# An RWKV scan in which VectorE adds the old state that identity products had loaded into PSUM

## The chip, the cores and the metric

The kernel runs on one core of a Trainium2 chip. The metric is the device time of one execution in microseconds (us), here the median of three runs. Five engines work beside each other, each in the order of its own program, and meet at semaphores: TensorE (PE in the profile; PEld is its loading of weights), VectorE (DVE), ScalarE (ACT), GpSimd (POOL) and SyncE (SP), which issues the transfers. [...]

## The reference

The program is one layer of a hybrid block: normalised and modulated tokens (256 context tokens, then 256 latent ones, width 2048) go through a projection, two token mixers (RWKV-7 and GLA), a gated merge, and a feed-forward part. The change is in the RWKV scan, 16 heads of 64 channels, once forward and once backward. Step by step it is

```python
def step(s, inp):
    sa = einsum('bhvk,bhk->bhv', s, kk_t)
    s = s * w_t - sa[..., None] * (kk_t * a_t) + v_t[..., None] * k_t
    return s, einsum('bhvk,bhk->bhv', s, r_t)        # the output, for latent tokens only
```

The latent scans start from the context scans' final states.

## The kernel before

The kernel is a row of blocks, each with a program for every engine, and a block starts when all engines are through with the one before. The scan is one block (`phase_rwkv_scan`); the mix and the feed-forward part follow in the next.

The scan works on chunks of 64 tokens, 8 for each direction: chunks 0 to 3 are context, 4 to 7 latent. A *half* is one chunk of one direction (`_f` forward, `_b` backward), all 16 heads; there are 16 halves, taken forward, backward, forward, and so on. A half of the context goes through these steps, a latent half through some more:

- `prepare` to `prepare3` (VectorE, with exponentials `es`, `e` from ScalarE): running sums of log decays (`b`) and the scaled operands `s12`, `q12`.
- `scores1`, `scores2`, `scores3`: products of them on TensorE (into `pb`, `pa`, `pb`; the third, wide one is for latent halves only, L1707), masked by VectorE into `first`, `t2` and `r12` (the page calls these `t_f`, `r_f`).
- `open`, four `stage`s and `close`: the inverse of a triangular matrix by doubling. In each, VectorE transposes (`turned`, L1457) and masks (`step`, L1459), ScalarE copies (`grown`), and TensorE multiplies (`grow`, L1737).
- `inverse`, `rhs`, `u`: TensorE forms the inverse, the right side (from the old state `S`) and their product u (L1780); ScalarE copies each (L1603 the right side, L1608 u).
- `from_state`, `output` (L1789, L1800, latent halves): the output in `pb`, copied into `b_y` by ScalarE or, in the last chunks, added to it by VectorE (L1516).
- `state`: the new state. Before the change, `u_step` first issues two products of the unit matrix with `S` (L1775) into the second half of each bank of `pa`; the state product (L1810) adds to them there; VectorE multiplies the whole by the decay over the chunk, `e_end` (L1507), and writes `S`.

The order of each engine is written out by hand. In `run_tensor`, `run_vector` and `run_scalar` a loop over n goes through the halves, and a line such as `latents("state", 2)` does that step for half n − 2 if it is a latent one (`context` and `every` likewise). So an engine works on two or three halves in turn, and a step waits for its semaphores with all that stands behind it on its engine. `ends` makes `e_end`; `forward` makes `e`.

Of the kernel before, what the change touches and what calls it, by code (L numbers as in the profile page):

```python
# [20 lines left out]
P = 128  # L21
# [5 lines left out]
C = 64  # L27
# [1207 lines left out]
def phase_rwkv_scan(nc, A, out, env, y_sum, yb, raw):  # L1235
# [3 lines left out]
    U8 = PAIRS  # L1239
# [3 lines left out]
    def sm(name, d):  # L1243

        if (name, d) not in names:
            names[name, d] = sem(f"s_{name}_{'fb'[d]}")
        return names[name, d]

    with ExitStack() as st:
# [126 lines left out]
        with nc.Block() as block:  # L1376
# [31 lines left out]
            def _(dve):  # L1408
# [108 lines left out]
                def run_vector(step):  # L1517
                    for n in range(-1, len(HALVES) + 3):
                        every, context, latents = calls(step, n)
                        latents("close", 3)  # L1520
                        context("stage", 2, 1)
                        latents("open", 2)
                        latents("prepare1", 1)
                        every("prepare2", 1)
                        context("stage", 2, 2)
                        latents("stage", 2, 1)
                        every("prepare", 0)
                        latents("stage", 2, 2)
                        latents("output", 3)
                        context("stage", 2, 3)  # L1530
                        latents("prepare3", 1)
                        latents("stage", 2, 3)
                        every("state", 3)
                        latents("scores1", 1)
                        context("stage", 2, 4)
                        context("scores1", 1)
                        latents("stage", 2, 4)
                        every("scores2", 1)
                        context("open", 1)
                        latents("scores3", 1)  # L1540
                        context("close", 2)
                        context("prepare1", 0)
# [4 lines left out]
            def _(act):  # L1547
# [61 lines left out]
                def run_scalar(step):  # L1609
                    for n in range(-1, len(HALVES) + 3):  # L1610
                        every, context, latents = calls(step, n)
                        every("u", 2)
                        context("stage", 1, 3)
                        context("prepare", -1)
                        latents("stage", 1, 2)
                        latents("output", 2)
                        context("stage", 1, 4)
                        latents("prepare", -1)
                        context("close", 1)
                        context("tokens", 0)  # L1620
                        latents("stage", 1, 3)
                        context("flips", 0)
                        context("forward", -1)
                        latents("stage", 1, 4)
                        latents("forward", -1)
                        context("ends", 0)
                        latents("close", 1)
                        latents("tokens", 0)
                        context("stage", 0, 1)
                        latents("flips", 0)  # L1630
                        every("halve", 1)
                        every("rhs", 1)
                        latents("ends", 0)
                        context("stage", 0, 2)
                        latents("stage", 0, 1)
# [14 lines left out]
            def _(pe):  # L1650
# [1359 lines left out]
```

## Time and profile before

| | |
|---|---|
| median of 3 runs | 2209.29 us (2205.83 to 2209.69) |
| profiled execution | 2204.9 us, span 2203.3 us |
| scan block | 966.6 to 1246.0 us of the span |
| context halves, about | 976.6 to 1096 us |
| latent halves, about | 1096 to 1231 us, then a tail |
| granted TensorE clock, mean | 0.966 |

The span is the profiled execution from its first to its last instruction. Times in the rows count from its start. A recorded group such as "MATMUL ... x32" is a run of products of one line: 16 products of 64 columns, which the trace shows as two each in this type.

### The profile page before, as it was taken

What the parts mean: (1) busy time and instruction counts of PE and PEld (TensorE: products, weight loads), DVE (VectorE), ACT (ScalarE), POOL (GpSimd) and SP (SyncE); (2) the same over time, 40 slices, a digit from 0 to 9 for tenths busy, and PEclk for the clock granted to TensorE, in tenths of its full rate; (3) what the DMA queues carried; (4) which work ended last, traced back from release to release, by engine and by line L of the source; (5) the groups of instructions that cost most, each with busy time, mean ns of one, the idle gap of its engine ahead of it and who ended that gap; (6) DMA issues with size and microseconds to landing.
All of it is one profiled execution on the core that took longest, in us unless ns stands there. A gap on an engine that the chain in (4) does not pass through costs nothing. (4 is left out here: it accounts for less than half of the span.)

```text
span 2203.3 us, 37509 instructions
## 1 busy us (share of the span) xinstructions
PE 2052.1 (93%) x16171; PEld 1691.6 (77%) x16171; DVE 1344.8 (61%) x1258; ACT 811.2 (37%) x890; POOL 277.2 (13%) x135
## 2 busy tenths in 40 slices
PE   7679999999899999977889899989999999999998
PEld 3258888888678886656778688878888888878886
DVE  3465666665627737768888677475656565654444
ACT  1232212123063125625555555343434334333333
POOL 0242213223113304411000020000000000000000
PEclk9689999999989999989999999999999999999999
DMA  9989888987173459997544477535555555555553
GB/s 333 348 285 328 306 323 283 328 309 229 40 221 95 108 145 267 311 244 177 104 89 85 58 230 299 193 105 191 190 190 190 190 187 187 179 206 195 191 191 115
DMA packets 406658, 454.09 MB, mean 206 GB/s; under 512 B 108062, under 2 KB 357262, under 8 KB 389246
## 3 DMA queue, kind: packets, MB, share of 16 engines
q1 hardware_dynamic: 398912, 441.04, 62.5%
q10 hardware_dynamic: 7614, 11.10, 1.4%
q8 instruction: 105, 1.72, 0.3%
q14 instruction: 27, 0.22, 0.0%
HBM read 413.89 MB, written 38.22 MB: 205 GB/s over the span
## 5 line engine op out<-in xcount | busy, mean ns | idle before, releaser
L215 DVE TENSOR_TENSOR f_w_lo<-t_w_raw,f_w_hi 128x2048 fp32r<-128x2048 f32 x132 | 302.3, 2290 | 307.0 <-ACT f_w_hi L209 307.0
L270 PE MATMUL pf<-h,f_w_hi 128*128 128x512 f32 x1320 | 463.9, 395 | 0.0
L209 ACT ACTIVATE f_w_hi<-t_w_raw 128x2048 fp32r<-128x2048 f32 x132 | 253.2, 1918 | 445.7 <-PE pf L270 283.6
L269 PE MATMUL pf<-h,f_w_lo 128*128 128x256 f32 x1320 | 367.4, 278 | 0.3 <-DVE h L2666 0.3
L270 PEld LDWEIGHTS pf<-h,f_w_hi 128*128 128x128 f32 x1320 | 247.6, 188 | 54.3
L269 PEld LDWEIGHTS pf<-h,f_w_lo 128*128 128x128 f32 x1320 | 248.3, 188 | 4.6 <-DVE h L2666 0.6
L209 ACT ACTIVATE p_w_hi<-h_w_raw 128x2048 fp32r<-128x2048 f32 (+1 forms) x52 | 96.4, 1901 | 338.8 <-DVE stage L726 252.1
L261 PE MATMUL p_in<-h,p_w_lo 128*128 128x512 f32 (+1 forms) x512 | 199.3, 389 | 0.0
L259 PE MATMUL p_in<-h,p_w_hi 128*128 128x512 f32 (+1 forms) x512 | 199.3, 389 | 0.0
L260 PE MATMUL p_in<-h,p_w_hi 128*128 128x512 f32 (+1 forms) x512 | 199.2, 389 | 0.0
L858 DVE SCALAR_TENSOR_TENSOR late_acc<-h_of_x,siluc,late_acc 128x2048 f32<-128x2048 f32 x60 | 161.9, 2698 | 38.5 <-DMA h_of_x<-in_ada_w 36.9
L2885 PE MATMUL d_out<-f_w_hi,hid 128*128 128x512 f32 x704 | 177.4, 392 | 2.9 <-DVE f_w_lo L215 2.9
L215 POOL TENSOR_TENSOR p_w_lo<-h_w_raw,p_w_hi 128x2048 fp32r<-128x2048 f32 (+1 forms) x26 | 123.5, 4753 | 312.5 <-ACT p_w_hi L209 312.5
L2885 PEld LDWEIGHTS d_out<-f_w_hi,hid 128*128 128x128 f32 x704 | 132.7, 189 | 31.2 <-DVE f_w_lo L215 3.6
L904 PE MATMUL po<-h_of_x,gate_w 128*128 128x256 f32 x576 | 133.1, 389 | 2.3 <-ACT g_vt L1995 0.9
L904 PEld LDWEIGHTS po<-h_of_x,gate_w 128*128 128x128 f32 x576 | 110.9, 196 | 19.6 <-issue 2.3
L260 PEld LDWEIGHTS p_in<-h,p_w_hi 128*128 128x128 f32 (+1 forms) x512 | 95.7, 187 | 20.6
L261 PEld LDWEIGHTS p_in<-h,p_w_lo 128*128 128x128 f32 (+1 forms) x512 | 95.7, 187 | 20.4
L259 PEld LDWEIGHTS p_in<-h,p_w_hi 128*128 128x128 f32 (+1 forms) x512 | 95.7, 187 | 20.3
L270 PE MATMUL p_in<-h,p_w_hi 128*128 128x512 f32 x300 | 106.3, 397 | 0.0
L215 DVE TENSOR_TENSOR m_w_lo<-t_w_raw,h 128x2048 fp32r<-128x2048 f32 x32 | 74.8, 2348 | 47.0 <-ACT h L209 47.0
L904 PE MATMUL r_pg<-h_of_x,gate_w 128*128 128x256 f32 x416 | 94.7, 384 | 7.1 <-DMA gate_w<-in_w_in 4.1
(408 smaller groups left out, 3332.1 us busy)
## 6 DMA issues: line engine op xcount, KB each, us to landing
h_of_x<-in_ada_w SPq DMA_DIRECT2D x64, 1024.0 KB, 5.0
h_w_raw<-in_w_in SPq DMA_DIRECT2D x51, 1024.0 KB, 7.2
t_w_raw<-in_ffn_w_gate SPq DMA_DIRECT2D x44, 1024.0 KB, 5.0
t_w_raw<-in_ffn_w_up SPq DMA_DIRECT2D x44, 1024.0 KB, 5.1
t_w_raw<-in_ffn_w_down SPq DMA_DIRECT2D x44, 1024.0 KB, 4.9
h_w_raw<-in_ada_w SPq DMA_DIRECT2D x32, 1024.0 KB, 8.8
gate_w<-in_w_in SPq DMA_DIRECT2D x32, 1024.0 KB, 5.8
t_w_raw<-in_w_out SPq DMA_DIRECT2D x16, 1024.0 KB, 6.3
```

The lines of the kernel that those rows point to most:

```text
L209: act.activation(self.hi[:, m % self.S, 0:w], self.raw[:, s, 0:w], ACT.Copy)\
L215: eng.tensor_tensor(self.lo[:, m % self.S, 0:w], self.raw[:, s, 0:w], b32(self.hi[:, m % self.S, 0:w]), ALU.subtract)\
L259: pe.matmul(o, wh, xh, start=first, stop=False)
L260: pe.matmul(o, wh, xl, start=False, stop=False)
L261: return pe.matmul(o, wl, xh, start=False, stop=last)
L269: pe.matmul(hi, wl, x[:, 0, k, :], start=False, stop=False)
L270: return pe.matmul(both, wh, x[:, :, k, :], start=False, stop=last)
L858: dve.scalar_tensor_tensor(out=acc, in0=self.raw[:, t % 2], scalar=scalar, in1=acc, op0=ALU.mult, op1=ALU.add).then_inc(self.used, 1)
L904: mm = pe.matmul(self.banks[t % nb][:, 0:SEQ], self.raw[:, slot, k * P:(k + 1) * P], self.hx[:, k, :], start=k == 0, stop=k == KT - 1)
L2885: return pe.matmul(pd[4 * b + c][:], hid[:, part, t, b * P:(b + 1) * P], v[:, t % 2, 512 * c:512 * c + 512], start=first, stop=stop)
```

## The change

Three things change. (1) `u_step` no longer issues the identity products; the state product starts its sums anew (`start=True`), and VectorE first adds the old state to it (`S` + `pa` into `S`, with a new semaphore `sadd`), waits for that, and then multiplies `S` by `e_end`. (2) `scores2`, which writes `pa`, waits for the addition and not for the multiplication. (3) The steps of the three compute engines are written in a new order. For most halves this gives the same order as before, since the loop's turn starts at another step (the numbers of halves back are shifted with it).

```diff
@@ state (VectorE) @@
                     dve.wait_ge(sm("st", d), c + 1)
+                    dve.tensor_tensor(by_parity(S[d][:]), by_parity(S[d][:]), narrow(pa[d], 1), ALU.add).then_inc(sm("sadd", d), 1)
+                    dve.wait_ge(sm("sadd", d), c + 1)
                     dve.wait_ge(sm("e_end", d), c + 1)
-                    dve.tensor_tensor(by_parity(S[d][:]), narrow(pa[d], 1), e_end[d][:].rearrange("p (u b) -> p b u", b=2)
-                                      .unsqueeze(3).broadcast_to([P, 2, U8 // 2, C]), ALU.mult).then_inc(sm("S", d), 1)
+                    dve.tensor_tensor(S[d][:], S[d][:], e_end[d][:].unsqueeze(2).broadcast_to([P, U8, C]), ALU.mult)\
+                       .then_inc(sm("S", d), 1)
@@ scores2 (TensorE) @@
-                        pe.wait_ge(sm("S", d), c)
+                        pe.wait_ge(sm("sadd", d), c)
@@ u_step (TensorE) @@
                     pe.wait_ge(sm("inverse", d), c + 1)
-                    goes_on = c != LAST
-                    if goes_on:
-                        for b in range(2):
-                            at = b * BANK + BANK // 2
-                            pe.matmul(pa[d][:, at:at + BANK // 2], eye[:],
-                                      S[d][:].rearrange("p (u b) c -> p b u c", b=2)[:, b], start=True, stop=False,
-                                      skip_group_check=True)
                     pe.wait_ge(sm("rhsc", d), c + 1)
...
-                        last = pe.matmul(by_token(pa[d], j, h), tok(xt[d], j, h), tok(rhs[d], j, h), start=not goes_on,
-                                         stop=True, skip_group_check=True)
+                        last = pe.matmul(by_token(pa[d], j, h), tok(xt[d], j, h), tok(rhs[d], j, h), start=True, stop=True)
@@ state (TensorE) @@
                         last = pe.matmul(by_feature(pa[d], j, h, 1), st12[d][:, 2 * j + h, :], uv[d][:, block_of(j, h), :],
-                                         start=False, stop=True, skip_group_check=True)
+                                         start=True, stop=True)
@@ run_tensor, two of its lines @@
-                        latents("grow", 1, 3)
-                        latents("scores2", 0)
...
+                        latents("scores2", -1)
...
+                        latents("grow", 0, 3)
@@ run_scalar, two of its lines @@
-                        latents("output", 2)
...
-                        latents("prepare", -1)
...
+                        every("prepare", -1)
...
+                        latents("output", 2)
```

On VectorE, in the context halves, the order stays but for the state. The piece is from a forward half: `pa` is the PSUM tile with the new state's product, `turned_b` and `step_b` belong to the next half, which is backward.

```order
 L1457 STREAM_TRANSPOSE turned_b<-pa 128x512
 L1459 TENSOR_TENSOR step_b<-turned_b,masks 128x512
-L1507 TENSOR_TENSOR S_f<-pa,e_end_f 128x2x4x64
+L1506 TENSOR_TENSOR S_f<-S_f,pa 128x2x4x64
+L1509 TENSOR_TENSOR S_f<-S_f,e_end_f 128x512
 L1457 STREAM_TRANSPOSE turned_b<-pb 128x512
 L1459 TENSOR_TENSOR step_b<-turned_b,masks 128x512
```

One instruction has become two, and the fourth transpose stands behind both.

On VectorE, in a latent half, before (`q_f` is the scaled operand of the half ahead, `first_f` its first selection):

```order
L1457 STREAM_TRANSPOSE turned_b<-pa 128x512
L1459 TENSOR_TENSOR step_b<-turned_b,masks 128x512
L1454 TENSOR_TENSOR q_f<-rc_f,e_f 128x8x64
L1507 TENSOR_TENSOR S_f<-pa,e_end_f 128x2x4x64
L1473 COPY_PREDICATED first_f<-masks,pb 128x512
L1457 STREAM_TRANSPOSE turned_b<-pb 128x512
```

and now:

```order
L1454 TENSOR_TENSOR q_f<-rc_f,e_f 128x8x64
L1457 STREAM_TRANSPOSE turned_b<-pa 128x512
L1459 TENSOR_TENSOR step_b<-turned_b,masks 128x512
L1506 TENSOR_TENSOR S_f<-S_f,pa 128x2x4x64
L1509 TENSOR_TENSOR S_f<-S_f,e_end_f 128x512
L1473 COPY_PREDICATED first_f<-masks,pb 128x512
```

The addition stands between the third mask and the first selection. (The scaling of `q_f` is in front of the transpose here, at the first latent half; in the later ones it was so before.)

On TensorE, from the right side of a latent half on, before (L1737 is the growth, L1689 the first scores, L1697 the second, L1707 the third):

```order
L1766 MATMUL pb<-S_b,q_b 64x64 x16
L1737 MATMUL pa<-first_f,step_f 64x64 x16
L1775 MATMUL pa<-S_b,ident 128x256 x2
L1780 MATMUL pa<-rhs_b,xt_b 64x64 x16
L1737 MATMUL pb<-grown_f,step_f 64x64 x16
L1810 MATMUL pa<-uv_b,st_b 64x64 x16
L1737 MATMUL pa<-grown_f,step_f 64x64 x16
L1689 MATMUL pb<-s_b,q_b 64x64 x16
L1737 MATMUL pb<-grown_f,step_f 64x64 x16
L1697 MATMUL pa<-q_b,s_b 64x64 x16
L1707 MATMUL pb<-q_b,s_b 128x64 x16
```

and now:

```order
L1772 MATMUL pb<-S_b,q_b 64x64 x16
L1743 MATMUL pa<-first_f,step_f 64x64 x16
L1779 MATMUL pa<-rhs_b,xt_b 64x64 x16
L1743 MATMUL pb<-grown_f,step_f 64x64 x16
L1808 MATMUL pa<-uv_b,st_b 64x64 x16
L1743 MATMUL pa<-grown_f,step_f 64x64 x16
L1695 MATMUL pb<-s_b,q_b 64x64 x16
L1703 MATMUL pa<-q_b,s_b 64x64 x16
L1743 MATMUL pb<-grown_f,step_f 64x64 x16
L1713 MATMUL pb<-q_b,s_b 128x64 x16
```

The identity products are gone, and the second scores have moved ahead of the third growth. In context halves TensorE's order loses the identity products and is otherwise the same. On ScalarE, `forward` stands earlier and `ends` later in context halves, and in latent halves `prepare` (the exponential `es`) has moved ahead of the second copy and the output's copy.

## Rows read from the trace of the kernel before

**Rows 1.** The page: the chain that ended last, share of the span by line.

```profile
PE pf L270 13%; PE d_out L2885 11%; PE pf L269 7%; PE o_out L2799 3%; PE m_up L270 1%; DMA t_w_raw<-in_w_gla_up 1%; PE pf L267 1%; PE m_up L269 1%; DVE m_w_lo L215 1%; PE pf L268 0%; ACT f_w_hi L209 0%; DVE f_w_lo L215 0%; PE o_turned L2839 0%; DMA t_w_raw<-in_ffn_w_gate 0%; ACT h L209 0%
```

**Rows 2.** Busy time by window: the whole scan, context stage, latent stage.

```profile
core 0: us, PE busy (x) PEld busy (x) DVE busy (x) ACT busy (x) POOL busy (x), PEclk, DMA share, GB/s
966.60:1246.00 279.40, 232.68 (x7160) 205.50 (x7160) 222.69 (x323) 141.19 (x246) 7.71 (x4) 0.95 0.51 107
976.60:1096.00 119.40, 92.97 (x2977) 80.29 (x2979) 99.05 (x138) 64.99 (x114) 6.72 (x2) 0.93 0.69 150
1096.00:1231.00 135.00, 120.85 (x3878) 109.22 (x3877) 111.88 (x159) 69.52 (x122) 0.00 (x0) 1.00 0.37 72
```

**Rows 3.** Timeline of one context half: start, duration, instructions, idle before and releaser.

```profile
start us, us, engine line op out<-in xcount [idle before <-releaser]
1046.05 0.71 DVE L1457 STREAM_TRANSPOSE turned_f<-pa 128x512 f32<-128x512 f32 x1
...
1047.76 0.60 ACT L1603 ACTIVATE rhs_b<-pb 128x512 f32<-128x512 f32 x1
...
1048.16 1.13 PE L1775 MATMUL pa<-S_b,ident 128*128 128x256 f32 x4
...
1049.22 1.09 PE L1780 MATMUL pa<-rhs_b,xt_b 64*64 64x64 f32 x30
1049.73 1.22 DVE L1431 TENSOR_TENSOR_SCAN b_f<-keep,ld_f 128x512 f32<-128x512 f32 x1
...
1050.42 1.21 ACT L1608 ACTIVATE uv_b<-pa 64x512 f32<-64x512 f32 x2 [0.70 <-PE pa L1780]
1050.99 0.72 DVE L1457 STREAM_TRANSPOSE turned_f<-pa 128x512 f32<-128x512 f32 x1
...
1051.77 1.15 PE L1810 MATMUL pa<-uv_b,st_b 128*64 128x64 f32 x32 [0.93 <-ACT uv_b L1608]
...
1052.98 0.69 DVE L1507 TENSOR_TENSOR S_b<-pa,e_end_b 128x512 f32<-128x512 f32 x1 [0.55 <-PE pa L1810]
...
1053.69 0.72 DVE L1457 STREAM_TRANSPOSE turned_f<-pb 128x512 f32<-128x512 f32 x1
...
1059.79 0.71 DVE L1457 STREAM_TRANSPOSE turned_b<-pa 128x512 f32<-128x512 f32 x1
```

**Rows 4.** Timeline of one latent half.

```profile
1192.79 0.69 DVE L1459 TENSOR_TENSOR step_b<-turned_b,masks 128x512 f32<-128x512 f32 x1
...
1193.79 0.27 PE L1737 MATMUL pb<-grown_b,step_b 64*64 64x64 f32 x2
...
1194.36 1.10 PE L1789 MATMUL pb<-q_f,S_f 64*64 64x64 f32 x32
...
1195.58 0.69 PE L1800 MATMUL pb<-r_f,uv_f 128*64 128x64 f32 x14
...
1196.85 0.74 PE L1800 MATMUL pb<-r_f,uv_f 128*64 128x64 f32 x18 [0.59 <-issue]
...
1197.63 0.69 DVE L1516 TENSOR_TENSOR b_y<-b_y,pb 128x512 f32<-128x512 f32 x1 [1.51 <-PE pb L1800]
...
1198.83 0.71 DVE L1457 STREAM_TRANSPOSE turned_b<-pa 128x512 f32<-128x512 f32 x1
...
1199.58 0.69 DVE L1459 TENSOR_TENSOR step_b<-turned_b,masks 128x512 f32<-128x512 f32 x1
1200.19 0.68 DVE L1507 TENSOR_TENSOR S_f<-pa,e_end_f 128x512 f32<-128x512 f32 x1
...
1200.79 0.73 DVE L1473 COPY_PREDICATED first_f<-masks,pb 128x512 f32<-128x512 uint32 x1
...
1201.58 2.00 PE L1707 MATMUL pb<-q_f,s_f 64*128 64x64 f32 x32
```

**Rows 5.** TensorE's waits, 976 to 1246: us in total, times, longest.

```profile
PE pb L1689 <- issue: 8.7, 5, 4.5
```

**Rows 6.** Busy time in one window, columns as in rows 2.

```profile
1024.00:1028.00 4.00, 3.55 (x80) 3.43 (x80) 2.74 (x4) 0.78 (x2) 2.23 (x1) 0.50 1.09 348
```

More of the change, by code:

```diff
@@ L1611, in run_scalar @@
                         every, context, latents = calls(step, n)
-                        every("u", 2)
+                        latents("rhs", 2)
+                        context("ends", 1)
+                        latents("stage", 1, 1)
+                        context("stage", 1, 2)
+                        context("u", 2)
                         context("stage", 1, 3)
-                        context("prepare", -1)
+                        latents("u", 2)
+                        every("prepare", -1)
+                        context("stage", 1, 4)
+                        context("forward", -1)
                         latents("stage", 1, 2)
                         latents("output", 2)
-                        context("stage", 1, 4)
-                        latents("prepare", -1)
+                        latents("stage", 1, 3)
+                        latents("ends", 0)
+                        latents("stage", 1, 4)
+                        latents("close", 1)
+                        latents("forward", -1)
                         context("close", 1)
+                        latents("tokens", 0)
+                        latents("flips", 0)
                         context("tokens", 0)
-                        latents("stage", 1, 3)
                         context("flips", 0)
[L1623 to L1628, printed above, removed]
                         context("stage", 0, 1)
-                        latents("flips", 0)
                         every("halve", 1)
[L1632 to L1635, printed above, removed]
+                        context("rhs", 1)
                 run_scalar(dict(prepare=prepare, forward=forward, ends=ends, output=output,
@@ L1815, in run_tensor @@
                         every, context, latents = calls(step, n)
-                        context("grow", 1, 2)
-                        latents("grow", 1, 1)
-                        latents("from_state", 2)
-                        latents("output", 2)
-                        context("state", 2)
-                        latents("grow", 1, 2)
-                        latents("state", 2)
-                        latents("scores1", 0)
-                        context("grow", 1, 3)
-                        context("scores1", 0)
-                        context("scores2", 0)
-                        latents("grow", 1, 3)
-                        latents("scores2", 0)
-                        latents("scores3", 0)
                         context("grow", 1, 4)
@@ L1837, in run_tensor @@
                         latents("flips", 0)
-                        every("inverse", 1)
-                        every("rhs", 1)
+                        context("inverse", 1)
+                        context("rhs", 1)
+                        latents("inverse", 1)
+                        latents("rhs", 1)
                         context("grow", 0, 1)
@@ L1842, in run_tensor @@
                         every("u", 1)
+                        latents("grow", 0, 1)
+                        latents("from_state", 1)
+                        context("grow", 0, 2)
+                        context("state", 1)
+                        latents("output", 1)
+                        latents("grow", 0, 2)
+                        latents("state", 1)
+                        latents("scores1", -1)
+                        context("grow", 0, 3)
+                        latents("scores2", -1)
+                        context("scores1", -1)
+                        latents("grow", 0, 3)
+                        context("scores2", -1)
+                        latents("scores3", -1)
                 run_tensor(dict(scores1=scores1, scores2=scores2, tokens=tokens, flips=flips, scores3=scores3,
```

27 lines of the change are left out of this document (15 added, 12 removed).

## Prediction

> **What bounds the kernel now.** I read the last chain first. Its largest pieces are products of the feed-forward part, and no line of the scan stands in it [rows 1]. That does not make the scan free: the phases are separate blocks, each waits for the one before it, and the chain reaches back only to the block behind the scan. Whatever the scan gives or takes goes on one to one. The scan is 279.4 us long, from 966.6 to 1246.0 (the bounds of its stages are those of [rows 2], with 10 us of start in front and 15 us of tail behind).
>
> Next the busy times by stage. In the context stage TensorE is busy for 92.97 of 119.40 us and VectorE for 99.05; in the latent stage TensorE for 120.85 of 135.00 and VectorE for 111.88 [rows 2]. Neither engine is full, so I need the order within a half (one chunk of one direction), and read the timeline of one half in each stage.
>
> In the context half, the reader should see that VectorE has one real pause, 0.55 us before it forms the state at 1052.98, and that from 1053.69 to 1059.79 it goes from one instruction to the next for 6.10 us without a listed wait. TensorE pauses 0.93 us for ScalarE's copy of u. The half takes 13.74 us, 1046.05 to 1059.79 [rows 3]. In the latent half TensorE runs nearly without a pause up to the output product; VectorE waits 1.51 us for that product. Then comes a tight stretch: third transpose 1198.83, its mask 1199.58, state 1200.19, first selection 1200.79, and TensorE's wide product at 1201.58, which needs that selection and on whose end VectorE's next masking waits [rows 4].
>
> **The change, part by part.** *The identity products go.* In both halves they hold TensorE for 1.06 us (1048.16 to 1049.22) before the u product; 14 of 16 halves have them, 14.8 us of TensorE in all. What is late next is the copy of the right side on ScalarE, which u needs. Context: it ends at 1047.76 + 0.60 = 1048.36, and with the 0.14 us that lies between ScalarE's end and TensorE's start elsewhere (1050.42 + 1.21 to 1051.77) u starts at 1048.50, 0.72 earlier, not 1.06 [rows 3]. In the latent half I take the same 0.7 us for u; there, as will be seen, it is not u that decides.
>
> *VectorE gets an addition in 14 halves.* Its form is not in the scan's state step before, but the same shape with one operand in PSUM is in the output sum at 1197.63, 0.69 us [rows 4]. What counts is start to start. Behind an instruction whose result is not needed at once the next starts 0.60 to 0.61 us later (1199.58 to 1200.19 to 1200.79); where the next needs the result it is 0.75 us (1198.83 to 1199.58) [rows 4]. The multiplication needs the sum, so the added price is 0.75 us of VectorE. The bounds are 0, if it lies in the 0.55 us pause and that pause was longer than it looks, and 0.75. I take 0.75, since an instruction of this kind has never cost less than 0.60 here. The multiplication now reads SBUF alone; the mask at 1199.58 does too and takes 0.69 us, the state from PSUM 0.68 [rows 4], so nothing changes.
>
> The Trainium skill (VectorE: DVE Perf Modes, "The DRAIN you can't avoid") says that a semaphore after each VectorE operation costs nothing over one after the last. These rows do not agree: 0.75 against 0.61 where the result is waited for. By the rule the addition would cost 0.61 and the sum below would be up to 1 us lower.
>
> *Context half, walked through.* u at 1048.50 ends at 1049.6; the copy of u starts when ScalarE is through with what stands before it, 1049.72 (1050.42 less the 0.70 of idle), and ends at 1050.93; the state product starts at 1051.07 and is 0.70 earlier. VectorE: second mask and scan stay, since they waited for TensorE's first growth, not for u. The third transpose moves from 1050.99 to 1050.95. Its mask starts at 1051.70, the addition at 1052.31 (the state product has ended at 1052.22), the multiplication at 1053.06, the fourth transpose at 1053.67. Before it was at 1053.69 [rows 3]. The 0.55 us pause has been turned into the addition, and what follows is VectorE's full 6.10 us. Gain: 0.02 to 0.04 us a half; over 7 halves 0.3 us. TensorE's saving has become waiting.
>
> *Latent half, walked through.* This half has a stop within TensorE's output product (0.59 us listed); without it the product, 1.15 us long where it runs through as the state product of the same shape does [rows 3], would have ended at 1196.73 and not at 1197.59, and the work behind it stood 0.86 us earlier: third transpose at 1197.97, wide product at 1200.72 [rows 4]. After the change the growth behind u, before at 1193.79, waits for VectorE's mask, which ends at 1193.48, so it starts at 1193.54, 0.25 earlier only; the product from the old state at 1194.11, output at 1195.33, third transpose 1197.72, all 0.25 gained. Then mask 1198.47, addition 1199.08, multiplication 1199.83, first selection 1200.44, which ends at 1201.17. The wide product starts at 1201.22 where it would have stood at 1200.72: 0.50 later, the addition's 0.75 less the 0.25. TensorE's new order adds no more: the second scores, now ahead of the third growth, wait for the addition's end (1199.77), start at 1199.8, growth at 1200.4, both done by 1201.1. But this uses up all the room there was. From the wide product on, VectorE's masking, transposes and scaling follow one another up to the next half, so 0.50 is the price of a half. The seven halves in which an addition meets latent scores make +3.5 us.
>
> *The other moves.* ScalarE has pauses of 0.7 us before the copy of u in the context half [rows 3]; moving the exponentials and the end decays fills such pauses. DMA triggers hang on the same steps as before. Where the stages meet, VectorE's scaling is placed ahead of a transpose, once; 1.2 us at most, in either direction. I count zero.
>
> **Sum.** −0.3 + 3.5 = +3.2 us. The profiled execution took 2204.9 us (span 2203.3 and 1.6 around it), so it would be 2208.1. The profiled one lies 4.4 us below the median 2209.29 of the runs shown; on the median the forecast is 2212.5. About 0.2%, or 4.4 us, is what a measurement of this kernel can tell from no change, so the likeliest outcome is the same or barely slower.
>
> **Rivals.** *A: TensorE sets the latent half and the addition hides (faster).* For it: 120.85 of 135 us busy [rows 2], and TensorE's stops within its own products, 8.7 us at the first scores alone, one of them 4.5 [rows 5]. The new wait for the addition comes right behind those scores, and a stop there would vanish in it. Against: the walk. Price: 7 × 1.06 = 7.4 us gained, 2201.9; with the other 4.2 us of those stops 2197.7.
>
> By the Trainium skill (Runtime: NRT & Kernel Launch, "Instruction fetch mechanics") fetching instructions is hidden behind their issue. Rows with a product broken off in its middle and no engine to wait for [rows 4, 5] do not fit that; by the rule the 4.2 us would not be there to gain.
>
> *B: VectorE sets every half (slower).* One mechanism: ScalarE's copy of u does not come the 0.7 us earlier, so the 0.55 us pause before the state stays and the addition is put behind it. Price 14 × 0.75 = 10.5 us, 2219.8. It decides as soon as the state product in the context half starts no earlier than before. For it: VectorE is the fuller engine of the context stage. Against: the copy had been waiting 0.70 us for TensorE.
>
> *C: TensorE's clock falls more often (slower).* In 1024 to 1028 the granted clock was 0.50, that is 1.2 GHz, and 80 products took 3.55 us, behind 4.5 us without products [rows 5, 6]. With identity products gone, TensorE idles more in the context stage. At 2.4 GHz the same work takes half of 3.55 us, so such a stretch costs 1.8 us; two falls of two such stretches each make 7.1 us, 2216.4, and three 2219.9. Against: pauses of 0.5 us in the regular halves did not bring it.
>
> **Chances.** The forecast 0.43 (its own range 2208 to 2216), A 0.24, B 0.16, C 0.12, stops moved to other places by the shorter program 0.05, either way. Faster by over 0.2%: A and half the last, 0.26. Slower: B, C, and the upper edge of the forecast, 0.36. The same: 0.38. Range 2201 (most of A) to 2221 (B).
>
> **What would show it.** Step by step, in the profile after: the addition about 0.69 us and 0.75 us ahead of the multiplication; context halves of 13.7 us with no pause before the state; TensorE pausing 0.5 us before the second growth in them; in latent halves the wide product 3.5 us behind the third transpose (2.75 before) and TensorE waiting for the addition before the second scores. A pause before the addition would speak for B, latent halves a microsecond shorter for A, more stretches at 0.50 for C. The forecast is wrong if the scan is more than 5 us off 282.6 us.

## The result, and the profile after

The changed kernel took 2216.57 us (median of 8 runs, 2210.53 to 2225.08), the kernel before 2209.32 on the same chip: ratio 1.0037, 95% interval 1.0022 to 1.0052. It is slower by 7 us; the forecast was 2212.5, inside a range of 2201 to 2221. The time lies in the range, but 0.6 us above the 2208 to 2216 that the forecast itself was given: the range reached so far up for the sake of the rivals. The profiled execution took 2214.55 us (span 2212.8), 9.6 us more than that of before. Of this some 2.4 us is the choice of executions, since that of before was quicker than all eight that were timed, 4.4 us below their median, and this one is 2.0 below its own. The scan grew from 279.4 to 289.7 us, so it explains all of it, and it lies 7.1 us off the 282.6 that the sum gave: by the prediction's own bound of 5 us the sum was wrong in this execution.

The same stages as in [rows 2], shifted with the scan's start and end:

```profile
core 0: us, PE busy (x) PEld busy (x) DVE busy (x) ACT busy (x) POOL busy (x), PEclk, DMA share, GB/s
965.30:1255.00 289.70, 225.28 (x7104) 201.07 (x7105) 235.38 (x337) 142.01 (x247) 7.71 (x4) 0.94 0.50 103
975.30:1097.20 121.90, 86.56 (x2921) 75.10 (x2921) 106.81 (x144) 64.92 (x114) 6.72 (x2) 0.93 0.67 147
1097.20:1238.90 141.70, 119.92 (x3877) 109.86 (x3881) 116.45 (x166) 70.30 (x122) 0.00 (x0) 0.96 0.36 69
```

TensorE is busy 7.4 us less over the scan and VectorE 12.7 us more (14 additions of 0.69 are 9.7 of that); the context stage grew by 2.5 us, the latent stage by 6.7, and there the granted clock fell from 1.00 to 0.96.

A context half, to be held against [rows 3] (from the first transpose of `pa` on):

```profile
start us, us, engine line op out<-in xcount [idle before <-releaser]
1047.55 0.71 DVE L1457 STREAM_TRANSPOSE turned_f<-pa 128x512 f32<-128x512 f32 x1
...
1050.02 1.15 PE L1779 MATMUL pa<-rhs_b,xt_b 64*64 64x64 f32 x32 [0.28 <-ACT rhs_b L1608]
...
1052.37 0.69 DVE L1457 STREAM_TRANSPOSE turned_f<-pa 128x512 f32<-128x512 f32 x1
1052.55 1.15 PE L1808 MATMUL pa<-uv_b,st_b 128*64 128x64 f32 x32 [0.48 <-ACT uv_b L1613]
...
1053.76 0.69 DVE L1506 TENSOR_TENSOR S_b<-S_b,pa 128x512 f32<-128x512 f32 x1
...
1054.48 0.69 DVE L1509 TENSOR_TENSOR S_b<-S_b,e_end_b 128x512 f32<-128x512 f32 x1
...
1055.09 0.71 DVE L1457 STREAM_TRANSPOSE turned_f<-pb 128x512 f32<-128x512 f32 x1
```

This is as walked through: the pause before the state is gone, the addition takes 0.69 us and stands 0.72 ahead of the multiplication (0.75 assumed), and the fourth transpose comes 7.54 us after the first, against 7.64 before. The half is 13.65 us long (1047.23 to 1060.88 between the starts of its `eyes` product), before 13.75.

One context half has something else in it, which the prediction did not look at. GpSimd there converts and subtracts the other mixer's output, in before at the same time to 0.01 us, and two instructions of VectorE that read SBUF alone, the new multiplication and a mask, take 2.36 and 4.25 us instead of 0.69. Each ends 0.5 us behind one of GpSimd's:

```profile
1019.42 1.89 POOL L1650 CAST yb<-b_gla 128x2048 fp32r<-128x2048 f32 x1 [53.12 <-DMA b_gla<-gla_y_scratch]
...
1019.49 2.36 DVE L1509 TENSOR_TENSOR S_b<-S_b,e_end_b 128x512 f32<-128x512 f32 x1
...
1021.39 4.83 POOL L1652 TENSOR_TENSOR yb<-b_gla,yb 128x2048 fp32r<-128x2048 f32 x1
...
1022.51 4.25 DVE L1459 TENSOR_TENSOR step_f<-turned_f,masks 128x512 f32<-128x512 f32 x1
```

The transpose between them, which reads `pb` in PSUM (where TensorE's products are written), takes 0.70 as always. In before only a mask of 1.37 us falls into this time, because the multiplication was through at 1019.72, and VectorE then waited 3.27 us for TensorE. This half grew by 1.1 us between its `eyes` products (20.74 to 21.87).

A latent half, to be held against [rows 4]:

```profile
1217.90 0.71 DVE L1457 STREAM_TRANSPOSE turned_f<-pa 128x512 f32<-128x512 f32 x1
...
1221.12 1.15 PE L1798 MATMUL pb<-r_b,uv_b 128*64 128x64 f32 x32
...
1223.61 0.71 DVE L1457 STREAM_TRANSPOSE turned_f<-pa 128x512 f32<-128x512 f32 x1
1223.91 0.69 PE L1695 MATMUL pb<-s_b,q_b 64*64 64x64 f32 x32
...
1224.96 0.68 DVE L1506 TENSOR_TENSOR S_b<-S_b,pa 128x512 f32<-128x512 f32 x1
1225.67 0.69 DVE L1509 TENSOR_TENSOR S_b<-S_b,e_end_b 128x512 f32<-128x512 f32 x1
...
1225.69 0.69 PE L1703 MATMUL pa<-q_b,s_b 64*64 64x64 f32 x32 [1.09 <-DVE S_b L1506]
1226.21 0.65 PE L1743 MATMUL pb<-grown_f,step_f 64*64 64x64 f32 x32
1226.28 0.72 DVE L1473 COPY_PREDICATED first_b<-masks,pb 128x512 f32<-128x512 uint32 x1
...
1227.06 2.00 PE L1713 MATMUL pb<-q_b,s_b 64*128 64x64 f32 x32 [0.20 <-DVE first_b L1473]
```

Again each step is there: TensorE waits 1.09 us for the addition before the second scores, and the wide product starts 3.45 us behind the third transpose (3.50 forecast, 2.75 in [rows 4]). From first to third transpose it is 5.71 us; in the half of before in the same place of the program, 5.95, so 0.24 is gained where the sum had 0.25. In a half in which nothing else happens the terms are right. What the sum lacks is in the other halves. TensorE's waits show it, the list of [rows 5] for the scan of after (those on "issue" of over 0.6 us, that is stops within TensorE's own products with no engine to wait for):

```profile
engine line waited for: us in total, times, longest us
PE pa L1743 <- issue: 9.3, 7, 2.2
...
PE pb L1695 <- issue: 4.5, 2, 4.1
...
PE pb L1798 <- issue: 2.8, 2, 1.8
PE pa L1779 <- issue: 2.8, 3, 1.4
...
PE pa L1703 <- issue: 1.9, 2, 1.5
...
PE pb L1743 <- issue: 1.2, 2, 1.0
...
PE pa L1808 <- issue: 0.7, 1, 0.7
```

and of before, the two lines of growth (L1737) that stand beside the 8.7 us of [rows 5]:

```profile
PE pa L1737 <- issue: 3.4, 5, 1.7
...
PE pb L1737 <- issue: 1.1, 2, 1.0
```

The stops have left the first scores (8.7 us, now 4.5; in the latent stage 4.1, now none), behind which TensorE now waits anyway, and more of them lie in the growth products (4.5 us, now 10.5), on which VectorE's next transpose waits. Over all products they are 18.7 us before and 23.8 after. Three stops in the latent stage were followed by a fall of the clock, of which that stage had none before. The first:

```profile
1094.68 0.68 PE L1743 MATMUL pa<-grown_b,step_b 64*64 64x64 f32 x27 [0.21 <-DVE step_b L1459]
1097.53 0.33 PE L1743 MATMUL pa<-grown_b,step_b 64*64 64x64 f32 x5 [2.18 <-issue]
...
1100.64 1.08 PE L1703 MATMUL pa<-q_f,s_f 64*64 64x64 f32 x32
```

The growth breaks off after 27 of its 32 products for 2.18 us; three microseconds later the second scores take 1.08 us, which take 0.69 at 1225.69. The other two end at 1131.44 (1.82 us, within the output product L1798) and 1169.35 (1.68 us, within a growth), and in the windows behind them the granted clock is 0.71 and 0.57, mostly 1.2 GHz:

```profile
1134.40:1137.80 3.40, 3.40 (x116) 3.33 (x114) 2.74 (x4) 0.22 (x1) 0.00 (x0) 0.71 0.03 7
1171.00:1174.40 3.40, 3.40 (x108) 3.21 (x104) 2.49 (x5) 0.64 (x2) 0.00 (x0) 0.57 0.00 0
```

A stop of this length does not always bring a fall: behind one of 2.12 us that ended at 1206.36 the granted clock stayed at 1.00 (1206 to 1212).

What the stops wait for can be read from the trace's packets. TensorE's instructions come in blocks of 16384 bytes on the queue that the page calls "q8 instruction". The three stops above end at 1097.53, 1131.44 and 1169.35, and the block before each had landed at 1096.01, 1129.91 and 1167.88; the stop of 4.51 us in before ended at 1024.45, its block landed at 1023.05. So it is everywhere: in the fourteen profiles of this document TensorE has 235 stops of 0.3 us or more within the scan, and every one ends 1.2 to 1.7 us behind the landing of such a block, while the blocks follow each other every 4.6 to 5.0 us on average.

### The profile page after: what moved, and what is told of

Read it like the earlier page. It is cut to its first block and busy times, and to the rows that moved or that the text cites. A ratio compares the mean times of both kernels' runs of the same rounds, so it can differ in the third digit from the quotient of the medians.

```text
span 2212.8 us, 37426 instructions
## 1 busy us (share of the span) xinstructions
PE 2046.1 (92%) x16115; PEld 1685.5 (76%) x16115; DVE 1357.5 (61%) x1272; ACT 812.2 (37%) x890; POOL 278.8 (13%) x135
```

## The experiments

The expectations name three explanations for the time beyond the sum. **V**: only the chain of steps counts, and the price is VectorE's addition (in e1 with TensorE's stops for what is left over). **P**: the price is the new placing of the steps, of which TensorE's swap of second scores and growth is a part. **F**, from e5 on: TensorE's stops. Ratios are against the kernel before on the same chip, with 95% intervals, from 5 to 12 executions of each kernel. The expected times were written for the chip of the result, where the kernel before took 2209.3 us; it took 2211.0 on that of e1 to e4, 2214.0 for e5 to e8, 2212.6 for e9 to e11 and 2211.2 for e12, so what is compared is the ratio. "Third to wide" is the time from the third transpose to the wide product in a latent half without a stop in that stretch.

**e1: the addition, in the old order of steps.** The three `run_` functions are those of before; against the changed kernel:

```diff
-                        latents("scores2", -1)
...
+                        latents("grow", 1, 3)
+                        latents("scores2", 0)
```

> The addition on VectorE and no identity products, with all three engines' steps in the order of before. Theory V (the added time is VectorE's addition in the tight stretch of the latent halves, 0.50 us in seven halves, and what more there is comes from TensorE stopping within its own products): 3.5 to 8 us over before, 2213 to 2217. Theory P (the new placing costs the time, the addition is hidden): within 2 us of before, 2207 to 2211.

2219.00 us, 1.0036 (1.0021 to 1.0050). The same as the changed kernel, as V had it, third to wide 3.45 as well: in the old order the addition alone costs 0.70 us there.

**e2: the new order alone.** Identity products and multiplication from PSUM as before; against the kernel before:

```diff
+                        latents("scores2", -1)
...
-                        latents("grow", 1, 3)
-                        latents("scores2", 0)
...
+                        latents("grow", 0, 3)
```

> The identity products and the single multiplication of before, with the steps placed as in the changed kernel. Theory V: within 2 us of before, 2207 to 2211. Theory P: 4 to 8 us slower than before, 2213 to 2217.

2211.44 us, 1.0001 (0.9989 to 1.0013): by the time, nothing, again as V had it. But third to wide is 3.19, not 2.75. Without the addition the order costs 0.44 us in such a half; the time doesn't show it.

**e3: the changed kernel without the addition.** The old state is left out of the new one; the multiplication reads PSUM.

```diff
-                    dve.tensor_tensor(by_parity(S[d][:]), by_parity(S[d][:]), narrow(pa[d], 1), ALU.add).then_inc(sm("sadd", d), 1)
-                    dve.wait_ge(sm("sadd", d), c + 1)
```

> The changed kernel without the addition: the old state is left out of the new one, VectorE multiplies straight from PSUM, and there are no identity products either. Theory V: by the walk the fourth transpose of a context half comes 0.4 us earlier than before (7 halves, 2.8 us) and the wide product of a latent half 0.25 (1.8 us): 2204 to 2206, some 11 us under the changed kernel. Theory P: the placing stays, so it stays within 4 us of the changed kernel, 2212 to 2216.

2216.99 us, 1.0034 (1.0021 to 1.0048). V is missed here and P met: taking out all 14 additions gave nothing that can be measured. The timeline says why the walk saw too much in it:

```profile
1221.26 0.71 DVE L1457 STREAM_TRANSPOSE turned_f<-pa 128x512 f32<-128x512 f32 x1
...
1222.61 0.68 DVE L1507 TENSOR_TENSOR S_b<-pa,e_end_b 128x512 f32<-128x512 f32 x1
1223.21 0.73 DVE L1473 COPY_PREDICATED first_b<-masks,pb 128x512 f32<-128x512 uint32 x1
...
1223.35 0.69 PE L1701 MATMUL pa<-q_b,s_b 64*64 64x64 f32 x32 [1.09 <-DVE S_b L1507]
...
1223.87 0.65 PE L1741 MATMUL pb<-grown_f,step_f 64*64 64x64 f32 x32
...
1224.44 2.12 PE L1711 MATMUL pb<-q_b,s_b 64*128 64x64 f32 x32
```

The second scores must wait until `pa` has been read, and the third growth is queued behind them. Without the addition the selection is ready at 1223.94, but TensorE comes to the wide product at 1224.44: 3.18 behind the transpose. With the addition it is 3.45. So in the new order an addition costs at most 0.27 us a half, and the order the other 0.43; in the old order (e1) the addition costs all of it. That it is the swap within the new order is read from this timeline; no run moved the swap alone in a kernel without the addition.

**e4: the changed kernel with the third growth ahead of the second scores again.**

```diff
-                        latents("scores2", -1)
                         context("scores1", -1)
                         latents("grow", 0, 3)
+                        latents("scores2", -1)
```

> The changed kernel with one of its moves undone: in latent halves TensorE does the third growth before the second scores again. Theory V: the wide product waits for VectorE's first selection in either order, so nothing changes, 2215 to 2218. Rival: the growth, held behind the wait for the addition, is late for the fourth transpose: 0.3 to 0.5 us in each of seven halves, 2213 to 2214.

2221.36 us, 1.0048 (1.0034 to 1.0062). Third to wide stays 3.45: with the addition in place the selection sets it and the swap is hidden, in that much the forecast was right. The kernel is not shown to be slower than the changed one: 0.11%, with an interval of about 0.20 either way.

**e5: neither identity products nor addition, old order.** The old state is left out, as in e3.

```diff
-                    if goes_on:
...
-                            pe.matmul(pa[d][:, at:at + BANK // 2], eye[:],
-                                      S[d][:].rearrange("p (u b) c -> p b u c", b=2)[:, b], start=True, stop=False,
-                                      skip_group_check=True)
```

> The kernel before with one thing taken out: the identity products. The old state is left out of the new one; the steps stand in the order of before, and VectorE does nothing more than before. Theory F (without these products, which fill TensorE for 1.06 us with few instructions, TensorE stops longer within its other products for want of instructions, and its clock falls behind the longer stops): slower than before though there is less work, 2214 to 2219. Theory V (less work is at least not slower; the time of the changed kernel is the addition's): by the walk 4.6 us less than before, 2204 to 2208.

2215.40 us (12 runs), 1.0005 (0.9993 to 1.0018). Work is taken away from TensorE and nothing is added: the walk gave 4.6 us less, which the interval excludes; but that it is slower than before, as F expected, is not shown either. Third to wide is 2.74, so the chain is as short as before. V alone can't give this; the stops can:

```profile
PE pa L1737 <- issue: 8.4, 7, 1.7
PE pb L1689 <- issue: 3.8, 1, 3.8
...
PE pb L1737 <- issue: 3.4, 4, 1.5
```

There are 11.8 us of stops in the growth where before had 4.5, as in the changed kernel, and 25.7 in all products together for 18.7.

**e6: the changed kernel with the identity products put back, unused** (the state product starts the sums anew behind them).

```diff
                     pe.wait_ge(sm("inverse", d), c + 1)
+                    if c != LAST:
+                        for b in range(2):
+                            at = b * BANK + BANK // 2
+                            pe.matmul(pa[d][:, at:at + BANK // 2], eye[:],
+                                      S[d][:].rearrange("p (u b) c -> p b u c", b=2)[:, b], start=True, stop=True)
```

> The changed kernel with the identity products put back in their place, but their sums not used: the state product starts anew over them, and VectorE adds as in the changed kernel. Theory F: faster than the changed kernel by several us though it does more, 2210 to 2214. Theory V: as the changed kernel or slower, 2216 to 2224, since VectorE has the addition and TensorE the products as well.

2216.58 us (12 runs), 1.0017 (1.0004 to 1.0030), against 1.0037 for the kernel that does less. The difference is 0.20% with an interval of about 0.20 either way, worked out from the two, so it is just at the edge of being shown; its sign is that of F. The stops went back to the first scores (9.1 us, 4.5 in the changed kernel), and those of the growth fell from 10.5 to 8.1.

**e7 and e8: the kernels before and after with an eighth of the scan's loads** (outside chunks 0 and 4), so that less else moves while TensorE's instructions are loaded. The output is not the reference's. Of five loads, one:

```diff
-                    sp.dma_start(ld[d][:], dir_d[d, :, 0:U8, at:at + C])
+                    k = U8 if c in (0, 4) else 1
+                    sp.dma_start(ld[d][:, 0:k], dir_d[d, :, 0:k, at:at + C])
```

> The kernel before with an eighth of the scan's loads: in all chunks but the first of each stage only the first of eight units is loaded, so the rest keeps the values of the first chunk (the scaled operands are then made from a second, unscaled tile, so that they stay small). All steps and waits are as before. If TensorE's stops come from its instruction blocks queuing behind these loads, nearly all of the 10 us of stops in the latent halves go, and with them some 10 to 15 us of the scan: 2193 to 2200. If they come from something else, the time stays within 4 us of before.

> The changed kernel with the same small loads. With no stops to lengthen, what is left between this kernel and its partner is the walk on paper: +3.5 us in the latent halves and -0.3 in the context halves, so 2 to 5 us over the kernel before with small loads. Theory F expects that, down from the 7 us of the full kernels. If the difference stays at 7 us or more with the stops gone, the stops are not what made up the rest.

e7 2202.04 us, 0.9941 (0.9927 to 0.9954); e8 2204.80 us, 0.9961 (0.9947 to 0.9975). No instruction of a compute engine was removed, and the kernel before is 0.6% faster, some 12 us, as F expected. Loads and instruction queues between 976 and 1246, first of before and then of e7 (packets, MB, share of 16 engines):

```profile
q1 hardware_dynamic: 89492, 26.87, 47.6%
q8 instruction: 57, 0.93, 1.5%
```

```profile
q1 hardware_dynamic: 29454, 12.08, 18.8%
q8 instruction: 57, 0.93, 1.5%
```

and all stops of e7 in that stretch of over 0.6 us:

```profile
PE pa L1739 <- issue: 5.9, 7, 1.7
...
PE pb L1691 <- issue: 3.7, 4, 3.0
```

(The 12.08 MB hold 0.4 of the next block, since e7's scan ends at 1242.2.) The instruction blocks are the same 57, of 16 KB (0.93 MB by 57), and the stops fell from 18.7 us to 10.8, in the latent stage from 10.0 to 4.7, not nearly to nothing as expected; in the changed kernel from 23.8 to 10.9 (e8). With the landings of the blocks above this shows it for about half of the stops' time: they are instructions that come late because of data in flight. What holds the other half is open. Between e8 and e7 the difference is 2.8 us of medians, 4.4 us by the ratios (0.20%, about 0.19 either way); the sum had +3.2. The profiles agree in part: the mean latent halves are 16.34 and 16.62 us, times 7 is 2.0, but the whole scan of e8's execution is 1.0 us shorter than that of e7's. So where loads are small the forecast's sum fits the times; the one pair of profiles does not confirm it.

**e9 and e10: kernels before and after with the loads spread.** The second half of `s12` and the two halves of `kkv` each wait for a later growth level of the chunk before.

```diff
+                        if c and n:
+                            sp.wait_ge(sm("level", d), (c - 1) * GROW + 1)
...
+                    for a in range(2):
+                        if c:
+                            sp.wait_ge(sm("level", d), (c - 1) * GROW + 2 + a)
+                        sp.dma_start(kkv[d][:, a], shared_d[:, U8 * a:U8 * a + U8, at:at + C]).then_inc(sm("in_kkv", d), 16)
```

> The kernel before, its loads the same but not in one burst: SyncE sends the second half of s12 and the two halves of kkv one after the other, each behind a later growth level of the chunk before. Theory F (instruction blocks of TensorE queue behind the scan's loads): the stops in the latent stage fall from 10 us towards the 4.7 of the small loads, the time by 3 to 5 us, to 2204 to 2206. Theory V (stops are chance, only the chain of steps counts): 2209 to 2210, or later where a load now comes late.

> The changed kernel with its loads spread in the same way. If the excess over the forecast's +3.2 us is queueing of instruction blocks, this is 3 to 4.5 us above e9 (about 2208), with stops in the latent stage under 8 us (13.9 in the changed kernel). If the excess has another cause, it stays 7 us above e9.

e9 2216.42 us, 1.0016 (1.0001 to 1.0031); e10 2215.01 us, 1.0005 (0.9995 to 1.0015), 12 runs each. F's expectations for the time were missed in both. The DMA's strip over 1096 to 1231, first before and then e9 (each digit tenths of a fortieth):

```profile
DMA  0019900497001990009920099300990000000000
```

```profile
DMA  8300554724391064640344802449016370000000
```

The bursts are gone, and e9 has as many stops in the latent stage as before (10.2 us), fewer in the context (4.7 for 8.8). The changed kernel gained more: its stops fell from 23.8 us to 16.7, in the latent stage from 13.9 to 8.9 where under 8 was expected, and those of the growth from 10.5 to 4.9. So how tightly the loads come does count, in one kernel and stage more than in another. The spreading has a price of its own: VectorE's scan L1431 (here L1435) waits 4.3 and 4.9 us for its load in e9 and e10, 0.7 and 0.9 without it. All the same the changed kernel is faster with its loads spread, 1.0005 against 1.0037, a difference of 0.32% with about 0.18 either way, and it is no longer slower than its partner: −0.11%, about 0.18 either way. Most of what the change had cost went with the stops, as F has it, but the interval of this pair leaves out the sum's +3.2 us (0.14%).

**e11: the products `q1` and `q2` on GpSimd instead of VectorE,** in the kernel before.

```diff
-                    dve.tensor_tensor(q12[d][:, :, 0, :], kkv[d][:, 0], decays(d, 1), ALU.mult).then_inc(sm("q1", d), 1)
+                    pool.tensor_tensor(q12[d][:, :, 0, :], kkv[d][:, 0], decays(d, 1), ALU.mult).then_inc(sm("q1", d), 1)
```

> The kernel before, with the two products q1 and q2 of each half moved from VectorE to GpSimd, which is idle in the scan. If VectorE's work is on the path of the latent halves (rival B), a half ends up to 1.4 us earlier and the time falls by 5 to 10 us. If TensorE and the chain of growth set it, nothing changes: 2208 to 2210. Slower, if the products of GpSimd come too late for the second scores (over 4 us from the loads' landing).

2216.64 us, 1.0030 (1.0013 to 1.0047). A product takes 1.28 us there, and with 1.4 us less for VectorE in each latent half the latent stage is as long as before (148.85 us, before 148.97, over the same nine periods between `eyes` products), a half of the context without a stop 13.71 for 13.75. So VectorE's fill does not set these halves; the chain of transpose, mask and growth would, which is argued and not tested by itself. The context stage lost 4.5 us (97.2 us for 92.7 over six periods). The edit brings this about: in GpSimd's program the conversion and the subtraction now stand behind five halves of products, run from 1037.78 on, and meet VectorE's mask (2.08 us instead of 0.69) and its scan (5.55 instead of 1.22). TensorE waits 3.12 us for a mask behind them, and the granted clock is 0.55 from 1043 to 1053. The time of this run therefore says nothing on rival B; its latent stage does.

**e12: small loads, identity products, the new order.** Against e7:

```diff
+                        latents("scores2", -1)
...
-                        latents("grow", 1, 3)
-                        latents("scores2", 0)
```

> Identity products kept, no addition, the steps in the changed kernel's order, and an eighth of the scan's loads (so the output is not the reference's, as in the two kernels with small loads). Compared with those two (ratios 0.9941 for the kernel before, 0.9961 for the changed one). If the order's swap of second scores and growth is a price of its own, as the third transpose to wide product of 3.19 us in the kernel with the new order alone says, seven latent halves are 0.44 later each: 3.1 us, ratio 0.9955, and the addition proper adds only 0.26 a half on top (1.8 us). If the swap costs nothing and the addition is the whole price: 0.9941, and the wide product 2.75 us behind the third transpose.

2202.89 us, 0.9961 (0.9948 to 0.9974), third to wide 3.19: the first expectation by the interval, and equal to e8. e7 against e12 is 0.20%, about 0.19 either way, so where stops are few the new order alone has a price, just clear of its interval. e8 against e12 is 0.00%, also about 0.19 either way; the 1.8 us (0.08%) that the addition should add on top are too little to be told by it.

All of it in one table. Stops are those of the whole scan but its first 10 us, in the profiled execution; "scan" is that execution's.

| kernel | ratio | third to wide | stops: first scores | stops: growth | stops: all | scan |
|---|---|---|---|---|---|---|
| before | 1 | 2.75 | 8.7 | 4.5 | 18.7 | 279.4 |
| e2, new order | 1.0001 | 3.19 | 9.5 | 9.8 | 24.8 | 292.3 |
| e5, none, old order | 1.0005 | 2.74 | 3.8 | 11.8 | 25.7 | 285.8 |
| e3, none, new order | 1.0034 | 3.18 | 4.1 | 12.3 | 23.6 | 288.4 |
| e1, addition, old order | 1.0036 | 3.45 | 4.3 | 13.2 | 23.8 | 292.9 |
| after | 1.0037 | 3.45 | 4.5 | 10.5 | 23.8 | 289.7 |
| e4, growth first | 1.0048 | 3.45 | 3.8 | 12.9 | 24.2 | 294.4 |
| e6, unused identity | 1.0017 | 3.46 | 9.1 | 8.1 | 21.6 | 288.7 |
| e9, before, spread | 1.0016 | 2.74 | 2.3 | 8.4 | 14.9 | 286.7 |
| e10, after, spread | 1.0005 | 3.46 | 1.8 | 4.9 | 16.7 | 288.3 |
| e11, GpSimd | 1.0030 | 2.74 | 6.9 | 6.6 | 18.7 | 287.8 |
| e7, before, small loads | 0.9941 | 2.73 | 3.7 | 6.3 | 10.8 | 276.9 |
| e12, new order, small loads | 0.9961 | 3.19 | 5.1 | 4.0 | 11.8 | 276.9 |
| e8, after, small loads | 0.9961 | 3.46 | none | 4.3 | 10.9 | 275.9 |

(The profiled execution of e2 took 2224.26 us, 13 above the median of its twelve; its scan and stops are of that one.) Every kernel of full and unspread loads that keeps the identity products has 7 to 10 us of stops in the first scores, every one without them 4, so where the stops fall goes with TensorE's program, though each row is one execution. The sum of the stops does not give the time: e2 and e5 have the most and are among the fastest of the unspread kernels. No version that keeps all of the computation beat the kernel before.

## Why the prediction was right or wrong

**Right: the steps.** Addition 0.69 us long, 0.72 ahead of the multiplication; pause before the state gone, context half 0.1 shorter where nothing stops (the pause of 0.5 us forecast before TensorE's second growth came in two parts, 0.28 before u and 0.21 before the growth); second scores waiting for the addition; third to wide 3.45 against 3.50. Rival B (14 × 0.75) is out: its pause did not come back. From the addition to the multiplication, which awaits it, it is 0.71 and 0.72 us, from the multiplication to what follows it 0.61: less than the 0.14 us between them that was assumed. By the Trainium skill (VectorE: DVE Perf Modes, "The DRAIN you can't avoid") a semaphore after each operation costs nothing extra; in these rows it costs 0.10 to 0.11.

**Right, with one side not seen: "TensorE's new order adds no more".** It adds nothing beside the addition (e4: 3.45 either way). But the new order by itself costs 0.43 us (e2, e3), as the addition by itself costs 0.70 (e1), and e12 has a price of 0.20% in the time with no addition at all. The walk asked what the swap adds after the addition was in, and never the other way round. Undoing either alone therefore gains little: e3 (addition gone) 0.27 us a half, e4 (swap gone) none.

**Wrong: −0.25 a latent half up to the third transpose, and "stops moved to other places" at 0.05, either way.** This is the step that failed: the walk took one stop out of its half, priced the half without it, and put nothing for what the shorter program does to the stops of the others. That the time still fell in the range is not the sum's doing. Means of the seven latent halves, before and after: first to third transpose 6.09 and 6.68 us, third to wide 3.35 and 3.49, the whole 17.03 and 17.88. The part forecast to gain 0.25 lost 0.59; the part forecast to lose 0.75 lost 0.14, at least partly because before it already held stops of the first scores, which the new wait now covers. Rival A had seen exactly that cover, and counted 4.2 us for it; it did not ask where those stops would go. They went to the growth products, in the first part of the half. Seven halves × 0.85 are 6.0 of the scan's 10.3 us; by the periods between `eyes` products the rest is 1.3 at its start, 1.3 in the context stage, 1.0 at its end and 0.7 in the first latent periods.

**Wrong: "the multiplication now reads SBUF alone, so nothing changes", and the context stage at −0.3.** In the half beside GpSimd's work this multiplication took 2.36 us and pushed the mask behind it into the subtraction, where it took 4.25; that half accounts for 1.1 of the 1.3 us that the context stage lost. The other context halves are 0.1 shorter only where nothing stops.

**C, in part.** The clock did fall more often, three times in the latent stage, not in the context stage and not from the pauses of 0.5 us, but behind stops of 1.7 to 2.2 us. Products of 0.69 us took 1.08 to 1.13, not twice as long as C assumed. That is an estimate of 1.5 us of TensorE's work for one fall (behind the second stop four groups of products, from 1132.67 on, take 4.72 us together and 3.22 at full clock), 4.5 for three, of which an unknown part lies under VectorE's chain. C's price of 2216.4 for two such pairs is the measured time, but only by luck.

**What stays open.** How the measured 0.37% is split. The chain's +3.2 us fits the times where loads are small (e7, e8, e12), and F is borne out by the landings of the blocks, by e5 (work removed, nothing gained), e7 and e10, and at the edge by e6. But e2 pays 0.44 us a half and is as fast as before, e3 differs from e5 by 0.29% where the new order explains 3.0 us of 6, and the spread pair shows no price for the change at all. So with full loads each program's own pattern of stops moves the time by some 0.1 to 0.3%, as much as the change itself; the runs do not tell which of it a given edit will draw. That a stop ends with the landing of a block is shown; why the block comes late, and what it waits for in the small-load kernels, is not. By the Trainium skill (Runtime: NRT & Kernel Launch, "Instruction fetch mechanics") crossing a block boundary is mostly hidden. The 18.7 us of stops in before do not agree with that for a stage made of 64x64 products, nor does e7, 0.59% faster than before with the smaller loads.

## What to carry to other kernels

When two edits meet at one join (here VectorE's addition and TensorE's swap before the wide product), walk each alone as well as both: each can hide the other, so that undoing one proves nothing. Where the trace shows products broken off in their middle, list those stops by line before removing instructions from that engine; a shorter program moves them, and one that lay beside a wait may land in the chain. When an operand of VectorE moves from PSUM to SBUF, look at what GpSimd does at that time. A saving of 15 us of TensorE was worth nothing here even when nothing was paid for it (e5).

## What the runs showed of the hardware

- Each of the 235 stops of 0.3 us or more within TensorE's products, in the scans of fourteen profiles, ended 1.2 to 1.7 us behind the landing of an instruction block of 16384 bytes.
- These stops follow the data in flight: 18.7 us in the scan of before with 26.9 MB loaded, 10.8 us with 12.1 MB over the same time, the same 57 instruction blocks. Taking the bursts apart left them in the latent stage of before (10.0 and 10.2 us) and shortened them in that of the changed kernel (13.9 and 8.9).
- Two VectorE instructions of 128x512 with both operands in SBUF took 2.36 and 4.25 us instead of 0.69 while GpSimd converted and subtracted 128x2048 (1.89 and 4.83 us); a transpose that read PSUM in the same time took 0.70. In e11 a scan took 5.55 instead of 1.22.
- A stop of 1.7 to 2.2 us within a product of TensorE was followed three times by a stretch at 1.2 GHz, once (2.12 us) not; the 64x64 products, 0.69 us for 32, then took 1.08 to 1.13, the wide product 2.28 instead of 2.00.
- The same product of 128x512 takes 1.28 us on GpSimd and 0.69 on VectorE.
